# Routing and the first two experts of a fused two-layer kernel: router logits from unscaled rows, rows picked by products, tables moved across a stage border

## The reference

```python
mixed = concat([pool_out, rwkv_out]) @ w_out
h = layer_norm_2(ALPHA * x + mixed, ln1_g, ln1_b)        # (y - mu) * rstd * g + b
g_prob = softmax(h @ router_group + router_group_b)       # 4 groups, top 1
e_logits = h @ router_expert + router_expert_b            # 32 experts, 8 per group, top 2 in the group
weights = g_top_p * softmax(e_top_logit)
# every (token, expert) pair gets a row; rows of one expert stand together, in blocks of 128
hid = silu(xb @ exp_gate[e]) * (xb @ exp_up[e])           # xb: 128 rows of h; gate and up 1024 x 256
ys = (hid @ exp_down[e]) * wgt                            # down 256 x 1024
ffn = scatter-add of ys to the tokens
out = layer_norm_2(ALPHA * h + ffn, ln2_g, ln2_b)
```

## Time and profile before

| | us |
|---|---|
| median of 3 runs | 2757.88 (2754.03 to 2758.43) |
| the profiled execution, own time | 2758.4 |
| its span | 2756.6 |
| TensorE busy in the span | 2633.9 (96%) |
| VectorE busy | 1654.8 (60%) |
| DMA, mean over the span | 126 GB/s |

### The profile page before, as it was taken

The page is one execution under the profiler, slowest core; times in us unless marked ns, Lnnn a source line. Parts: engine busy times, 40 slices in busy tenths (PEclk is TensorE's granted clock), DMA queues, the critical chain, the costliest instruction groups (busy, mean ns, idle before and its releaser), DMA issues. The chain is left out here.

```text
span 2756.6 us, 54579 instructions
## 1 busy us (share of the span) xinstructions
PE 2633.9 (96%) x21544; PEld 1728.0 (63%) x21544; DVE 1654.8 (60%) x4437; ACT 725.2 (26%) x1770; POOL 311.0 (11%) x415
## 2 busy tenths in 40 slices
PE   6999989999999999999999999999999898899996
PEld 4888856664588644788544467777777555344443
DVE  5444267886555657665556378888888666322225
ACT  3211056651310000000000246655566300100002
POOL 0000033310000000000000001011111000733412
PEclk9999999999999999999999999999999998899998
DMA  6010044330022446123444410100000030899985
GB/s 247 32 62 31 1 143 164 123 119 36 31 77 92 143 163 217 73 79 121 153 168 168 157 63 29 29 10 22 29 29 3 20 124 31 317 399 399 401 342 198
DMA packets 108847, 347.51 MB, mean 126 GB/s; under 512 B 8753, under 2 KB 18481, under 8 KB 99521
## 3 DMA queue, kind: packets, MB, share of 16 engines
q1 hardware_dynamic: 100160, 319.00, 31.7%
q0 software_dynamic: 8448, 25.18, 2.5%
HBM read 311.05 MB, written 33.10 MB: 125 GB/s over the span
## 5 line engine op out<-in xcount | busy, mean ns | idle before, releaser
L2076 PE MATMUL mixing_ps<-all_main,pre_ws 64*64 64x256 f32 x3072 | 245.9, 380 | 0.0
L3093 PE MATMUL ex_ps<-all_main,ex_xT 128*128 128x512 f32 x512 | 232.0, 597 | 12.5 <-DVE ex_xT L3239 10.0
L1318 PE MATMUL mlp_ps<-mlp_w2s,all_main 128*128 128x512 f32 x512 | 239.6, 592 | 0.0
L1318 PE MATMUL mlp_ps<-all_main 128*128 128x512 f32 x384 | 183.2, 592 | 0.7 <-DVE all_main L1541 0.7
L3093 PEld LDWEIGHTS ex_ps<-all_main,ex_xT 128*128 128x128 f32 x512 | 95.2, 191 | 121.8 <-issue 118.1
L1318 PEld LDWEIGHTS mlp_ps<-mlp_w2s,all_main 128*128 128x128 f32 x512 | 96.6, 190 | 117.8 <-issue 105.6
L2076 PEld LDWEIGHTS mixing_ps<-all_main,pre_ws 64*64 64x64 f32 x3072 | 126.5, 134 | 27.2 <-issue 4.0
L254 PE MATMUL qkv_ps<-qkv_wq,h_hT 128*128 128x256 f32 x576 | 133.9, 385 | 2.9 <-DVE h_hT L547 2.9
L1318 PEld LDWEIGHTS mlp_ps<-all_main 128*128 128x128 f32 x384 | 72.7, 190 | 93.3 <-issue 69.9
L254 PEld LDWEIGHTS qkv_ps<-qkv_wq,h_hT 128*128 128x128 f32 x576 | 111.1, 193 | 19.6 <-issue 4.1
L1532 DVE TENSOR_TENSOR all_main<-mlp_w2s 128x512 f32<-128x512 f32 x64 | 44.3, 691 | 130.6 <-PE mlp_ps L1318 129.3
(11 more groups left out here) (483 smaller groups left out, 5050.6 us busy)
## 6 DMA issues: line engine op xcount, KB each, us to landing
mlp_w2s<-in_w SPq DMA_DIRECT2D x64, 1024.0 KB, 4.9
all_main<-in_w_gu SPq DMA_DIRECT2D x32, 2048.0 KB, 14.4
all_early<-in_w SPq DMA_DIRECT2D x32, 1024.0 KB, 4.8
att_wa<-in_w_ada SPq DMA_DIRECT2D x32, 512.0 KB, 3.9
all_early<-in_w_d SPq DMA_DIRECT2D x16, 1024.0 KB, 17.3
all_main<-in_w_d SPq DMA_DIRECT2D x16, 1024.0 KB, 17.2
y_rows<-ex_y SPq DMA_DIRECT2D x32, 512.0 KB, 9.5
qkv_wq<-in_w_qkv SPq DMA_DIRECT2D x6, 2048.0 KB, 7.6
```

The source lines that it names most:

```text
L1318: last = nc.tensor.matmul(ps[:, PRODUCTS.index(name), :], lhsT=lhsT, rhs=rhs, start=j == 0, stop=j == FPAIRS - 1)
L2076: last = nc.tensor.matmul(ps[heads(m), banks[half], 0:UT], lhsT=ws[heads(half), n, k, heads(m)], rhs=columns(k, heads(half)), start=(k == ...
L3093: last = nc.tensor.matmul(pg[:, n % 2, :], lhsT=xT[:, n % 2, k * P:(k + 1) * P], rhs=gu[n][:, k, :], start=(k == 0), stop=(k == KT - 1))
```

## The change

- `layer_norm_steps` writes the normalised row without gain and bias to a second buffer, `plain`, and signals it (`plain_ready`); `turn` turns `plain`. The router weights are multiplied by the gain once (`wg`), and the bias times the weights is summed once by eight products (`bias_row`) and added to the router's bias.
- The order in iteration t becomes: `mix` in pieces, `count(t-2)` after two products, `bias_row` (t = 1 only), `turn(t-1)`, `logits(t-1)`, `first_rows(t-2)` inside the same `mix`. VectorE does `normalise(t)`, `find_slot(t-1)`, `route(t)`.
- `find_slot` also writes selection matrices for the experts 0 and 1 (`first_slots`). After the last `mix`, TensorE multiplies each tile of h with them (`pick`, eight products of width 256 for each tile), which gives the rows of both experts already turned. ScalarE and VectorE copy them to where the gathered rows lay.
- The experts 2 and 3 are loaded by SyncE inside the first stage, once the last `mix` is done.
- The spread products and the conversion to `tok_of_row` move behind the border, and GpSimd gathers for experts 2 and 3 only. `p_hidden(0)` moves ahead of part of the tables; `diag` moves behind the pipeline.

```diff
 def layer_norm_steps(...)
-    done(nc.vector.tensor_scalar(src, src, mv[:, 0:1], mv[:, 2:3], ALU.subtract, ALU.mult))
-    done(nc.vector.tensor_tensor(src, src, g_row, ALU.mult))
+    nc.vector.tensor_scalar(plain, src, mv[:, 0:1], mv[:, 2:3], ALU.subtract, ALU.mult).then_inc(plain_ready, 1)
+    dve.wait_ge(plain_ready, n + 1)
+    done(nc.vector.tensor_tensor(src, plain, g_row, ALU.mult))
...
 SyncE, first stage
                 for t in range(TT):
+                    if t == TT - 1:
+                        sp.wait_ge(mm, TT)
+                        for n in range(AHEAD, len(gu)):
+                            sp.dma_start(gu[n], w_gu[n]).then_inc(g_in, 16)
+                            sp.dma_start(dn[n], w_d[n]).then_inc(g_in, 16)
                     sp.wait_ge(h_ready, t + 1)
                     sp.dma_start(h_dram[t * P:(t + 1) * P, :], hres[:, t, :]).then_inc(h_out, 16)
...
 TensorE, first stage
+                def pick(t):
+                    pe.wait_ge(h_ready, t + 1)
+                    pe.wait_ge(first_placed, PICKED * (t + 1))
+                    for k in range(KT):
+                        last = nc.tensor.matmul(ps[:, k // 2, ...], lhsT=hres[:, t, k * P:(k + 1) * P],
+                                                rhs=first_slots[:, t, :], ...)
+                    last.then_inc(picked, 1)
                 for t in range(1, TT):
                     if t >= 2:
                         pe.wait_ge(mm_taken, t - 1)
-                    mix(t, 0, range(KT))
-                    mix(t, 1, range(0, 4))
-                    turn(t - 1)
-                    mix(t, 1, range(4, KT)).then_inc(mm, 1)
-                    logits(t - 1)
-                    if t >= 3:
-                        first_rows(t - 3)
+                    mix(t, 0, range(0, 2))
                     if t >= 2:
                         count(t - 2)
+                    mix(t, 0, range(2, KT))
+                    if t == 1:
+                        bias_row()
+                    turn(t - 1)
+                    mix(t, 1, range(0, 2))
+                    logits(t - 1)
+                    mix(t, 1, range(2, 5))
+                    if t >= 2:
+                        first_rows(t - 2)
+                    mix(t, 1, range(5, KT)).then_inc(mm, 1)
+                count(TT - 2)
+                pe.wait_ge(mm_taken, TT)
+                pick(0)
+                pick(1)
                 turn(TT - 1)
+                pick(2)
                 logits(TT - 1)
-                first_rows(TT - 3)
-                count(TT - 2)
+                pick(3)
+                first_rows(TT - 2)
+                for t in range(4, TT - 1):
+                    pick(t)
                 count(TT - 1)
-                first_rows(TT - 2)
+                pick(TT - 1)
                 first_rows(TT - 1)
-                (the four spread products)
...
 VectorE, first stage
+                    for e in range(PICKED):     # in find_slot, 128x128 each
+                        ts(first_slots[:, t, e * P:(e + 1) * P], cnt[:, IOTA + 1:IOTA + 1 + P],
+                           ps[:, 7, ...], both[:, t, e:e + 1], ALU.is_equal, ALU.mult).then_inc(first_placed, 1)
...
+                find_slot(TT - 1)
+                dve.wait_ge(picked, TT)
+                for c in range(PICKED):
+                    nc.vector.tensor_copy(first_x[:, c, NB:D]..., picked_x[:, 4:8, c]).then_inc(right_turned, 1)
...
 second stage
+                for a in range(4):              # TensorE
+                    last = nc.tensor.matmul(plist[:, 0, ...], lhsT=routing.lane[:, a, :], rhs=routing.acc[:], ...)
+                last.then_inc(rows_spread, 1)
-                p_up_first(0, 0, 1)
-                up(pipe, 0, 0, REST)
+                up(pipe, 0, 0, range(KT), xg[:, 0, :])
+                dve.wait_ge(rows_spread, 1)     # VectorE
+                nc.vector.tensor_scalar(tok_of_row[:, :, 0:EXPERTS], plist[:, 0, ...], ...).then_inc(rows_known, 1)
+                nc.vector.tensor_copy(xT[:, 1, :], xg[:, 1, :]).then_inc(pipe.x_turned, 1)
+                pool.wait_ge(rows_known, 1)     # GpSimd
+                for n in range(PICKED, NW):
```

More of the change, by code:

```diff
@@ L2623, in _, with layer_norm_steps @@
                 dve.wait_ge(dve_y.sem, dve_y.at(UNITS - 1, "y_out"))
-def layer_norm_steps(nc, dve, src, stats, mv, g_row, b_row, n, done, root_ready, rooted):
+def layer_norm_steps(nc, dve, src, plain, stats, mv, g_row, b_row, n, done, root_ready, rooted, plain_ready):
     for c in range(2):
@@ L2781, in first_rows, with bias_row @@
                     last.then_inc(found, 1)
+                def bias_row():
+                    pe.wait_ge(folded, 2)
+                    for k in range(KT):
+                        last = nc.tensor.matmul(ps[:, 7, 0:LOGITS], lhsT=ones[:], rhs=wb[:, k, :], start=(k == 0), stop=(k == KT - 1))
+                    last.then_inc(bias_sum, 1)
+                def pick(t):
+                    pe.wait_ge(h_ready, t + 1)
+                    pe.wait_ge(first_placed, PICKED * (t + 1))
+                    for k in range(KT):
+                        last = nc.tensor.matmul(ps[:, k // 2, (k % 2) * PICKED * P:(k % 2 + 1) * PICKED * P], lhsT=hres[:, t, k * P:(k + 1) * P],
+                                                rhs=first_slots[:, t, :], start=(t == 0 and k % 2 == 0), stop=(t == TT - 1 and k % 2 == 1))
+                    last.then_inc(picked, 1)
                 pe.sem_inc(mm, 1)
@@ L2854, in normalise @@
                     dve.wait_ge(mm_taken, t + 1)
-                    layer_norm_steps(nc, dve, h, stats, mv, rows[:, 0, :], rows[:, 1, :], t, done, root_ready, rooted)
+                    if t >= 2:
+                        dve.wait_ge(turned, t - 1)
+                    layer_norm_steps(nc, dve, h, plain[:, t % 2, :], stats, mv, rows[:, 0, :], rows[:, 1, :], t, done, root_ready, rooted,
+                                     plain_ready)
                     dve.sem_inc(h_ready, 1)
@@ L3045, in gather @@
                                                      ).then_inc(x_in[n], 16)
-                for n in range(NW):
+                pool.wait_ge(rows_known, 1)
+                for n in range(PICKED, NW):
                     for a in range(4):
@@ L3090, in _, with up @@
             def _(pe):
[L3091 removed]
+                def up(ring, b, n, ks, x=None):
                     for k in ks:
[L3093 to L3094 removed]
+                        last = nc.tensor.matmul(pg[:, n % 2, :], lhsT=(xT[:, n % 2, :] if x is None else x)[:, k * P:(k + 1) * P],
+                                                rhs=gu[n][:, k, :], start=(k == 0), stop=(k == KT - 1))
                     if ks[-1] == KT - 1:
@@ L3142, in _ @@
                 pe.sem_inc(more.downed, 1)
-                p_up_first(0, 0, 1)
-                up(pipe, 0, 0, REST)
+                for a in range(4):
+                    last = nc.tensor.matmul(plist[:, 0, a * EXPERTS:(a + 1) * EXPERTS], lhsT=routing.lane[:, a, :], rhs=routing.acc[:],
+                                            start=True, stop=True)
+                last.then_inc(rows_spread, 1)
+                up(pipe, 0, 0, range(KT), xg[:, 0, :])
                 with pe.Fori(0, EXPERTS // NW - 1) as j:
@@ L3363, in _ @@
                     p_take_y(b, b, b // 2 + 1)
+                for t in range(TT):
+                    for c in range(2):
+                        nc.vector.tensor_scalar(diag[:, c, t, :], ident[:], wgt[:, c, t:t + 1], None, ALU.mult).then_inc(weighed, 1)
                 dve.wait_ge(o_found, 1)
@@ L3500, in layouts_second, with chunk_rows @@
     }
+def chunk_rows(w):
+    return w.reshape(-1, P, w.shape[1]).transpose(1, 0, 2)
 def layouts_third(np, I):
@@ L3513, in layouts_third @@
         "w_d": I["exp_down_2"][0].reshape(EXPERTS, 2, P, D).transpose(0, 2, 1, 3),
+        "w_gu_first": np.stack([chunk_rows(gu[e]) for e in range(2)]),
+        "ln1_cols": np.stack([col(I["ln1_g_2"][0]), col(I["ln1_b_2"][0])], axis=1),
         "ln2": np.stack([I["ln2_g_2"][0], I["ln2_b_2"][0]]),
```

108 lines of the change are left out of this document (57 added, 51 removed).

## The result

The changed kernel is slower: 2764.65 us median of 9 runs (2759.67 to 2771.38) against 2755.92 of 9 runs of the kernel before (2753.10 to 2761.19), ratio 1.0032, 95% interval [1.0023, 1.0042]. The forecast was 2761 with a range from 2753 to 2767, and "within 0.2%" as the likeliest case; it is 0.3%.

The account below looks back on a forecast made before the run. TensorE was taken to bound the first stage and the experts' pipeline, with 35.86 us between them. 6.35 + 1.3 - 1.93 - 3.26 + 0.5 = +3.0 us; forecast 2761, range 2753 to 2767.

Parts of the forecast that it names:

- within 0.2%: Whole kernel: time within 5.5 us of 2757.9, about what a measurement can tell from no change; chance 0.56.
- To T0: First stage up to T0, when the last `mix` is done: +6.35 us, T0 at about 2326.7.
- T0 to S: From the last `mix` done (T0) to the first expert's `up` starting (S): 37.2 us instead of 35.86, +1.3.
- The picks, not the routing, set this: Behind the last `mix`: TensorE's queue is full until 29.3 us, while VectorE has routed the last tile at 19.4.
- I take it that the clock stays up: -1.93: First experts: TensorE, stopped only some 2.4 us at the stage border, keeps its full clock, saving 1.93 us.
- The first rival: Stage border: clock falls, spread products take 1.9 instead of 0.9 us, first experts lose 1.93; +2.9, 2763.9; chance 0.25.
- The waits for weights: Early experts' pipeline: loading experts 2 and 3 from the last `mix` on removes all waits for weights, -3.26 us.
- the second rival: Experts' pipeline: waits for weights stay, as DMA engines are at their 400 GB/s limit; +3.3 us, 2764.3; chance 0.07.
- `diag`: Behind the last expert: its 3.3 us, less 2.8 us in which VectorE was waiting there, cost +0.5 us.

## Why the prediction was right and wrong

**To T0: right, term by term.** 6.40 us for 6.35: 3.41 at the bias row for 3.4 (the wait 1.60, the products 1.81), and 2.99 for 2.95 of logits and small products. Leaving the bias row out gave 3.36 back. The period stayed 17.29.

**T0 to S: right mechanism, 0.8 short.** "The picks, not the routing, set this" is shown by the kernel with one pick: 13.9 us less. A pick is 3.50 us, 28.0 for eight against 27.5; the border from VectorE's last instruction to the spread products took 1.14, not 0.7, and VectorE was done 0.3 later.

**"I take it that the clock stays up: -1.93": this step failed.** From S two experts' worth of work took 19.33 us (2362.56 to 2381.89), against 19.31 before: nothing was gained. I had weighed the stop of 2.37 us in the recurrence as evidence that such a stop alone is harmless; the same row also had the clock at 0.50 2.5 us later, and I put that down to further small gaps. Here there were none: after the stop of 2.42 the work was dense, and the clock fell all the same, behind the start of the work. With the stop cut to 0.90 it did not fall (6.95 us for `up(0)`, in two kernels). The first rival had the right place and, for the first experts, nearly the right price (1.95 for 1.93). Its other microsecond, slow spread products, did not come here (0.88 us); it came in the kernel with the bias row behind the turn. Its 2763.9 is what was measured within 0.8, by luck in good part: of its 2.9 us only 1.95 came, and terms that it did not have (0.8, 0.87 and 1.4) made up the rest, see below. The rule of the Trainium skill that was cited, that bursts of products with waits between them go cold again and pay at each burst ("TensorE: Matmul & The Clock Gate", "HAM oscillation — how this bites in real kernels"), agrees with the stop of 2.42 in direction. The waits in that page's example are longer than this stop, though, so it does not by itself give the first rival, though the prediction took it so. In the kernels that came to this border at the full clock, `up(0)` ran slow behind stops of 2.37, 2.41, 2.42 (three), 2.72 and 3.25 us, and at full rate behind those of 0.90 (two), 1.71 and 2.09 us.

**The waits for weights: -2.4, not -3.3.** The step was right in kind, but about a quarter of it did not come: 0.87 us is left of 3.26 in the changed kernel, and 0.65 with the early loads alone in the kernel before, which shows that the late start of these loads caused most of the waits. What is left may be the second rival in a small size, a pipeline that asks for 399 GB/s of 400; no run tests that.

**`diag`: right.** +0.25 for +0.5.

**Not foreseen: +1.4 at the end.** TensorE's clock is at its lower level when the weighed sums start, in all kernels; how long it stays there was 2.8, 5.4 and 6.1 us in the three traces (before, after, early loads alone). The kernel with early loads alone lost as much, so neither `diag` nor the picks are the cause. Whether the early loads are, or the one profile of the kernel before was lucky, stays open.

Sum over the prediction: 0.05 + 0.8 + 1.95 + 0.87 + 0.1 (rest of that stretch) - 0.25 + 1.4 = 4.9, which makes 7.9 of 3.0. The medians differ by 8.7. What the ninth microsecond is can't be read from one trace. The nine runs of the changed kernel stand in two clusters, 2759.7 to 2764.7 and 2768.3 to 2771.4 us, and so do those with the store moved, 2760.3 to 2762.0 and 2767.3 to 2771.4. The clusters differ in TensorE's granted clock, averaged over the execution: 0.985 to 0.986 in the lower ones, 0.982 to 0.984 in the upper ones. By an estimate, 0.003 less over 2762 us is 16.6 us more at the lower level, which costs 8.3 us where TensorE is the bound: about the distance of the clusters. So the slower executions had their clock down for longer somewhere. The fall behind the bias row's stop, 3.3 us in one profile, may be a part of that; where the rest is lost is open, and some of it may lie ahead of the changed code, as the first stage started between 2198.70 and 2206.76 us in the 14 profiles, and no edit touches the code ahead of it. Nor is a ratio of one group the same in the next: the changed kernel had 1.0032 and 1.0049, and 1.0028 with the store moved, so the 0.0024 (6.6 us) by which leaving out the bias row lowered it, where the trace moved by 3.4, may be no more than that.

**A better version.** With one expert picked, the picks (14.5 us) fit beside the routing of the last tile, which two (28) don't; together with the bias as one product and no stop before the picks this is 0.9959 [0.9946, 0.9973] to the kernel before, 10 us faster, and 0.007 below the changed kernel with its store moved, in the same group. That the additions to the single pick (0.9969 [0.9957, 0.9980] alone) give something is shown by the traces only, 3.4 us from the first `mix` to the end; the ratios don't tell them apart.

## What to carry to other kernels

When a product on TensorE takes the place of a transfer, compare its length with the chain of the other engines beside which it runs, not with the transfer: here 14 us fit and 28 set the end. Count a short stop at a stage border as a risk of a fallen clock even if dense work follows, and look for the fall behind the start of that work too: in the changed kernel it came 1.4 us after it. A load that is issued early has to end before whatever waits for its queue: list every transfer that a border waits for and add up their bytes.

## What the runs showed of the hardware

- Products of width 128 in fp32 with a new stationary block each took 0.115 us a record (1.84 us for 16), those of width 256 0.219: the price still halves with the width, unlike that of width 36 or 32 (0.106 a record in the logits).
- The granted clock fell to 0.50 after a stop of only 1.36 us, followed by narrow products, in one of the profiles, and not in the five others with the same code.
- Behind nearly the same stop of 2.41 to 2.42 us the granted clock fell 1.4 us after TensorE went on in the changed kernel (the spread products still in 1.05 us), and before it went on in the kernel with the bias row moved (clock 0.83 in the 2 us ahead of the restart, spread products in 1.88 us).
- SyncE's queue took four loads of 6.3 MB in all but blocked for 6.24 us on the fourth; what was queued behind it went out that much later.
- Gathered rows landed 5.0 us after their issue beside a 3 MB load, and within 1.9 us without it.
- The passage of the loop over overflow blocks (no product in it) left TensorE idle for 10.4 to 11.2 us on some chips and 14.1 to 14.9 on two others, on which the kernel before was about 4 us slower too.
